# A chunked RWKV-7 state recurrence (WKV) inside a two-layer network: small transposes moved onto quarters of the matmul array, and side work moved to other steps

## What is computed

```python
def step(S, inp):                       # per token t and head (32 heads of 64 channels)
    r_t, w_t, k_t, v_t, kk_t, a_t = inp
    sa = jnp.einsum('bhvk,bhk->bhv', S, kk_t)
    S = (S * w_t[:, :, None, :]
         - sa[..., None] * (kk_t * a_t)[:, :, None, :]
         + v_t[..., None] * k_t[:, :, None, :])
    y = jnp.einsum('bhvk,bhk->bhv', S, r_t)
    return S, y
...
    mu = jnp.mean(y, -1, keepdims=True)
    yc = y - mu
    var = jnp.mean(yc * yc, -1, keepdims=True)
    y = (yc * lax.rsqrt(var + GN_EPS)).reshape(B, T, C) * gn_g + gn_b
```

## Time and profile before

| | |
|---|---|
| time, median of 3 runs | 2222.34 us (2221.25 to 2223.14) |
| time of the profiled execution | 2224.67 us |
| its span, first to last instruction | 2222.9 us |
| PE busy | 2170.7 us (98%) |
| the 16 steps, from the first key product to the first matmul of the output projection | 1506.98 to 1612.07 us, 105.09 us |
| granted PE clock over the span | 0.992 |

### The profile page before, as it was taken

The page is one execution under the profiler, slowest core; times in us unless marked ns, Lnnn a source line. Parts: engine busy times, 40 slices in busy tenths (PEclk is TensorE's granted clock), DMA queues, the critical chain, the costliest instruction groups (busy, mean ns, idle before and its releaser), DMA issues.

```text
span 2222.9 us, 38422 instructions
## 1 busy us (share of the span) xinstructions
PE 2170.7 (98%) x14720; PEld 1853.2 (83%) x14720; DVE 1486.3 (67%) x2054; ACT 1080.1 (49%) x1520; POOL 89.0 (4%) x78
## 2 busy tenths in 40 slices
PE   9999999999999999999899999998899999999997
PEld 7888888888888888888788887887688888888886
DVE  6656568885578856885875589784676644566655
ACT  5444555444444444445644755544434534456533
POOL 0700000000000000000000000001210000000000
PEclk9999999999999999999999999999999999999998
DMA  8655545665666656655464555653454555654552
GB/s 291 206 160 159 166 150 177 189 188 185 187 188 188 189 188 189 189 170 175 148 214 146 172 164 160 202 161 81 109 182 146 179 180 191 194 154 143 165 186 86
DMA packets 399585, 383.35 MB, mean 172 GB/s; under 512 B 43497, under 2 KB 397345, under 8 KB 398625
## 3 DMA queue, kind: packets, MB, share of 16 engines
q1 hardware_dynamic: 399458, 381.58, 55.7%
HBM read 374.65 MB, written 6.87 MB: 172 GB/s over the span
## 4 chain that ended last, share of the span: by engine, by line
PE 87%; DVE 8%; ACT 2%; issue 2%; DMA 1%; POOL 0%; DVEq 0%; SPq 0%; ACTq 0%; POOLq 0%
PE acc L793 45%; PE acc L796 22%; PE acc L824 3%; PE acc L879 2%; PE acc L880 2%; PE acc L881 2%; DVE w_lo L2072 2%; PE acc L827 2%; PE aux L1165 1%; ACT w_hi L1448 1%; PE aux L1074 1%; PE aux L896 1%; PE aux L1094 1%; DVE inverse L2508 0%; PE aux L1373 0%
## 5 line engine op out<-in xcount | busy, mean ns | idle before, releaser
L2072 DVE TENSOR_TENSOR w_lo<-raw_w,w_hi 128x1024 fp32r<-128x1024 f32 (+1 forms) x592 | 712.8, 1223 | 458.0 <-ACT w_hi L1448 456.4
L1448 ACT ACTIVATE w_hi<-raw_w 128x1024 fp32r<-128x1024 f32 (+1 forms) x592 | 613.6, 1046 | 674.7 <-PE acc L796 576.1
L793 PE MATMUL acc<-h,w_hi 128*128 128x512 f32 x1664 | 525.8, 397 | 1.2 <-DVE w_lo L2072 1.2
L796 PEld LDWEIGHTS acc<-h,w_lo 128*128 128x128 f32 x1664 | 312.6, 188 | 73.8
L796 PE MATMUL acc<-h,w_lo 128*128 128x256 f32 x1664 | 327.0, 278 | 0.0
L793 PEld LDWEIGHTS acc<-h,w_hi 128*128 128x128 f32 x1664 | 254.5, 189 | 2.1 <-issue 1.3
L793 PE MATMUL acc<-ff,w_hi 128*128 128x512 f32 x704 | 222.8, 398 | 2.4 <-DVE ff L2329 2.4
L793 PE MATMUL acc<-x_split,w_hi 128*128 128x512 f32 x704 | 225.2, 401 | 0.0
L793 PE MATMUL acc<-xs_b,w_hi 128*128 128x512 f32 x512 | 162.5, 399 | 1.7 <-DVE w_lo L2517 0.9
L796 PEld LDWEIGHTS acc<-ff,w_lo 128*128 128x128 f32 x704 | 133.0, 189 | 31.5
L796 PEld LDWEIGHTS acc<-x_split,w_lo 128*128 128x128 f32 x704 | 132.2, 188 | 31.2
(11 more groups left out here) (370 smaller groups left out, 3100.2 us busy)
## 6 DMA issues: line engine op xcount, KB each, us to landing
raw_w<-in_w_up SPq DMA_DIRECT2D x176, 512.0 KB, 3.5
raw_w<-in_a_w_in SPq DMA_DIRECT2D x128, 512.0 KB, 3.8
raw_w<-in_w_in SPq DMA_DIRECT2D x64, 512.0 KB, 4.0
raw_w<-in_w_down SPq DMA_DIRECT2D x64, 512.0 KB, 3.6
raw_w<-in_b_w_qg SPq DMA_DIRECT2D x64, 512.0 KB, 3.7
raw_w<-in_w_o SPq DMA_DIRECT2D x32, 512.0 KB, 3.6
raw_w<-in_a_w_out SPq DMA_DIRECT2D x32, 512.0 KB, 3.8
raw_w<-in_w_k_shared SPq DMA_DIRECT2D x32, 512.0 KB, 4.5
```

The source lines that it names most:

```text
L793: pe.matmul(ACC[2 * b + f], WHI[:, q, k, f * P:(f + 1) * P], op[:, kt, :, :].rearrange("p h t -> p (h t)"), start=first, stop=False)
L796: mm = pe.matmul(ACC[2 * b + f][:, 0:T], WLO[:, slot, k, f * P:(f + 1) * P], op[:, kt, 0, :], start=False, stop=last)
L1448: act.activation(WHI[:, u % 4, 0:ku, :], RAWW[:, u, 0:ku, :], ACT.Copy).then_inc(hi_made, 1)
L2072: dve.tensor_tensor(WLO[:, u, 0:ku, :], RAWW[:, u, 0:ku, :], WHI[:, u % 4, 0:ku, :].bitcast(F32), ALU.subtract)\
```

## The change

The tile transposes are done head by head: eight 64x64 matmuls in place of four with 128 rows, each on a quarter of the array, the two heads of a tile into two banks. To make room the state's sums go to the banks of X and U, so `x_first` has to wait until the sums are read, and comes after the second term of Y. `turn_beta` follows `turn_k` at once. `group_squares` moves ahead of `beta_pairs`, DVE's reading of its sums ahead of the copy of U. Weight units are split in other steps, and one `head_pair` and one `by_gate` per group come one and two steps later.

```diff
--- before.py
+++ after.py
@@ -477,14 +477,15 @@
 ...
-        PAIR_BANKS, KB_BANK, V_BANK = BANKS[:, 0:2, :], BANKS[:, 2, :], BANKS[:, 3, 0:T]
-        STATE_SUMS = BANKS[:, 3, T:].rearrange("p (e x) -> p e x", e=2)
-        XU_BANKS, Y_BANKS = SIDE[:, 0:2, :], SIDE[:, 2:4, :]
+
+        PAIR_BANKS, KB_BANKS, V_BANKS = BANKS[:, 0:2, :], BANKS[:, 2:4, 0:T], BANKS[:, 2:4, 384:]
+        XU_BANKS, Y_BANKS, STATE_SUMS = SIDE[:, 0:2, :], SIDE[:, 2:4, :], SIDE[:, 0:2, 384:]
 
         def by_two(x):
 
             return x.rearrange("p e (j t) -> p e j t", j=2)
-        SPLIT_AT = [5, 9, 13, 14]
+        SPLIT_AT = [6, 10, 14, 14]
+        LOW_SPLIT_AT = [10, 14, 15, 15]
 
 ...
@@ -754,7 +755,7 @@
                 g, c = STEPS[n]
                 if c == 3 and 0 < g < 3:
                     by_gate(2 * (g - 1))
-                if c == 0 and g > 1:
+                if c == 2 and g > 1:
                     by_gate(2 * (g - 2) + 1)
                 if c == 0 and g:
                     pool.wait_ge(gn_sq_sum, g)
@@ -1156,14 +1157,14 @@
             channel, between = (lambda h_, e: (h_, e)), (lambda h_, e: (h_ ^ e, e))
             across = lambda h_, e: (1 - e, h_)
 
-            def quads(banks, at, lhs, rhs, place, start, stop, one_bank=False):
+            def quads(banks, at, lhs, rhs, place, start, stop):
 
                 for j in range(2):
                     for e in range(2):
                         for h_ in range(2):
                             b, bank = place(h_, e)
                             mm = pe.matmul(banks[64 * b:64 * b + 64, bank, at + j * CHUNK:at + (j + 1) * CHUNK], lhs(h_, 2 * j + e), rhs(h_, 2 * j + e),
-                                           start=(start and j == 0 and not (one_bank and e == 1)), stop=(stop and j == 1 and (e == 1 or not one_bank)))
+                                           start=(start and j == 0), stop=(stop and j == 1))
                 return mm
 
 ...
@@ -1233,31 +1234,28 @@
                                        start=(i < 2), stop=(i >= 2))
                 mm.then_inc(prep_done, 1)
 
-            def tile_of(x, n, i):
-                g, c = STEPS[n]
-                return x[:, 4 * g + i, c * CHUNK:(c + 1) * CHUNK]
+            def turn_heads(banks, x, n, half, unit_, place):
+
+                for j in range(2):
+                    for e in range(2):
+                        for h_ in range(2):
+                            a, b = place(2 * j + e), half ^ e
+                            mm = pe.matmul(banks[64 * b:64 * b + 64, h_, a:a + CHUNK], at(x, n)(h_, 2 * j + e),
+                                           unit_[64 * h_:64 * h_ + 64, 64 * h_:64 * h_ + 64], start=(j == 0), stop=(j == 1))
+                return mm
 
             def turn_v(n):
                 if n:
                     pe.wait_ge(vt_out, 2 * n)
-                for i in range(4):
-                    b = i % 2
-                    mm = pe.matmul(V_BANK[64 * b:64 * b + 64, i // 2 * P:(i // 2 + 1) * P], tile_of(V, n, i), CENTRE, start=(i < 2), stop=(i >= 2))
-                mm.then_inc(tok_done, 1)
-
-            def turn(x, n, half):
-                for i in range(4):
-                    b = half ^ i % 2
-                    mm = pe.matmul(KB_BANK[64 * b:64 * b + 64, i * P:(i + 1) * P], tile_of(x, n, i), IDENT, start=True, stop=True)
-                return mm
+                    pe.wait_ge(kb_out, k_beta_turned(n - 1))
+                turn_heads(V_BANKS, V, n, 0, CENTRE, lambda i: i // 2 * CHUNK).then_inc(tok_done, 1)
 
             def turn_k(n):
-                if n:
-                    pe.wait_ge(kb_out, k_beta_turned(n - 1))
-                turn(K, n, 0)
+                pe.wait_ge(vt_out, 2 * n + 2)
+                turn_heads(KB_BANKS, K, n, 0, IDENT, lambda i: i * CHUNK)
 
             def turn_beta(n):
-                turn(BET, n, 1).then_inc(tok_done, 1)
+                turn_heads(KB_BANKS, BET, n, 1, IDENT, lambda i: i * CHUNK).then_inc(tok_done, 1)
 
             def group_squares(g):
 
@@ -1290,6 +1288,8 @@
                 m = n % 2
                 pe.wait_ge(pairs_read, n + 1)
                 pe.wait_ge(vt_out, 2 * n + 2)
+                if n:
+                    pe.wait_ge(s_taken, 3 * (n // NCH) + n % NCH)
                 mm = quads(XU_BANKS, 0, tok(k_kappa(m)), v_tok(m), between, True, n % NCH == 0)
                 mm.then_inc(x_begun if n % NCH else x_done, 1)
 
@@ -1316,40 +1316,37 @@
                     turn_v(n + 1)
                 pe.wait_ge(us_ready, 3 * n + 1)
                 quads(XU_BANKS, T, cross, far(US), between, True, True).then_inc(w_done, 1)
+                if c == 0 and g:
+                    group_squares(g - 1)
                 if more:
                     beta_pairs(n + 1)
                 if n:
                     pe.wait_ge(y_out, n)
                 if c > 0:
                     quads(Y_BANKS, 0, state, at(R, n), channel, True, False).then_inc(s_read, 1)
-                elif g:
-                    group_squares(g - 1)
                 pe.wait_ge(ws_ready, n + 1)
                 quads(XU_BANKS, P, inverse, mid(XS), across, True, True).then_inc(u_done, 1)
                 if state_next:
                     turn_k(n + 1)
+                    turn_beta(n + 1)
                 pe.wait_ge(us_ready, 3 * n + 3)
                 if c < 3:
                     pe.wait_ge(kb_out, k_beta_turned(n))
                     pe.wait_ge(vt_out, 2 * n + 4)
-                    quads(STATE_SUMS, 0, kb(m), vu(m), channel, True, True, one_bank=True).then_inc(s_done, 1)
-                if c == 3 and more:
-                    x_first(n + 1)
-                if state_next:
-                    turn_beta(n + 1)
-                if c < 3:
-                    x_first(n + 1)
+                    quads(STATE_SUMS, 0, kb(m), vu(m), channel, True, True).then_inc(s_done, 1)
                 pe.wait_ge(rest_out, n + 1)
                 if c == 0 and g:
                     pe.wait_ge(gn_read, g)
                 quads(Y_BANKS, 0, vu(m), rho(m), channel, c == 0, True).then_inc(y_done, 1)
+                if more:
+                    x_first(n + 1)
 
             k_pairs(0)
             turn_v(0)
+            beta_pairs(0)
+            x_first(0)
             turn_k(0)
             turn_beta(0)
-            beta_pairs(0)
-            x_first(0)
             for n in range(len(STEPS)):
                 step(n)
 
@@ -1867,13 +1864,14 @@
             def v_copies(n):
                 act.wait_ge(tok_done, v_turned(n))
                 for e in range(2):
-                    act.activation(v_and_u(n % 2)[64 * e:64 * e + 64, :, e, :, :],
-                                   V_BANK[64 * e:64 * e + 64, :].rearrange("p (j h t) -> p j h t", j=2, h=2), ACT.Copy).then_inc(vt_out, 1)
+                    act.activation(v_and_u(n % 2)[64 * e:64 * e + 64, :, e, :, :].rearrange("p j h t -> p h j t"),
+                                   by_two(V_BANKS[64 * e:64 * e + 64, :, :]), ACT.Copy).then_inc(vt_out, 1)
 
             def k_beta_copy(n):
                 if n % NCH < 3:
                     act.wait_ge(tok_done, v_turned(n) + 1)
-                    act.activation(k_and_beta(n % 2), KB_BANK, ACT.Copy).then_inc(kb_out, 1)
+                    act.activation(k_and_beta(n % 2).rearrange("p (i h t) -> p h i t", i=4, h=2),
+                                   KB_BANKS.rearrange("p h (i t) -> p h i t", i=4), ACT.Copy).then_inc(kb_out, 1)
 
             def in_slots(x):
                 return x[:, :, :].rearrange("p (e j) t -> p e j t", e=2)
@@ -1907,8 +1905,8 @@
                     k_beta_copy(n + 1)
                 if c == 1 and g:
                     head_rstd(g - 1)
-                if n in SPLIT_AT:
-                    split_unit(SPLIT_AT.index(n))
+                for u in heads_at(n, SPLIT_AT):
+                    split_unit(u)
 
             v_copies(0)
             k_beta_copy(0)
@@ -2567,6 +2565,10 @@
                     read_kappa(n + 1)
                 dve.wait_ge(w_done, n + 1)
                 dve.tensor_tensor(slots(XS), by_two(XU_BANKS[:, :, T:384]), slots(XS), ALU.add).then_inc(ws_ready, 1)
+                if c == 0 and g:
+                    dve.wait_ge(gn_sq_sum, g)
+                    dve.tensor_scalar(GROWS[:, 0, :].rearrange("p (e t) -> p e t", e=2), Y_BANKS[:, :, P:T], 1.0 / CHUNK, GN_EPS,
+                                      ALU.mult, ALU.add).then_inc(gn_read, 1)
                 dve.wait_ge(u_done, 2 * n + 2)
                 dve.tensor_copy(v_and_u(n % 2)[64:P, :, 0, :, :].rearrange("p j h t -> p h j t"), by_two(XU_BANKS[64:P, :, P:T])).then_inc(us_ready, 1)
                 if more:
@@ -2590,14 +2592,11 @@
                         dve.wait_ge(s_taken, 3 * g + 1)
                         dve.sem_inc(s_ready, 1)
                 if c == 0 and g:
-                    dve.wait_ge(gn_sq_sum, g)
-                    dve.tensor_scalar(GROWS[:, 0, :].rearrange("p (e t) -> p e t", e=2), Y_BANKS[:, :, P:T], 1.0 / CHUNK, GN_EPS,
```

(7 more changed lines are left out.)

## The result

The changed kernel takes **2225.19 us** (median of 20 runs, 2220.49 to 2228.4) against 2222.62 for the kernel before in 20 runs beside it: a ratio of 1.0013 with a 95% interval of 1.0007 to 1.0019. It is 2.6 us slower where I forecast 5.7 us faster, and the time lies outside my range.

The account below looks back on a forecast made before the run. The recurrence was taken as bound by a chain passing between engines, which no engine fills. Step, side, start and end terms summed to 8.3 us gained, less 2.6 for two clock falls: 5.7 faster, 2216.6 us, range 2212.5 to 2220.5.

Parts of the forecast that it names:

- Prices of the parts: Unit costs on PE: an old turn issues in 0.42 to 0.46 us, a new one taken as 0.24, from `beta_pairs`.
- Ordinary steps: Eight steps with c = 0 or 1: second inverse product to x_second 2.72 us instead of 3.07, 2.8 gained.
- slower: Clock falls in ordinary steps, 1.3 us each; seven cancel the gain, one in each of 15 steps gives 2233.5; chance 0.04.
- Rival 3: New turns no cheaper, 0.43 us each: K's and beta's end later in 11 steps, 2.9 less gain, 2219.5; chance 0.10.
- Rival 2: PE's wait for its own last group costs 0.3 us more in 12 steps with x_second: 2220.2; chance 0.16.
- c = 2: Four steps without turns of K and beta: 2.75 us before, 2.72 after, 0.1 gained in all.
- The side terms: Gains from moved side work: sums' reading 1.1 us, `head_pair` 1.3, roots and splits 0.6 and 1.7, clock 1.3.
- the clock of step 6: Granted clock of 0.53 for 3.41 us after step 6's long idle; it goes with the idle, 1.3 us gained.
- Step 3 to 4: Second inverse product to the next: 4.88 us instead of 5.45, 0.6 gained.
- End: After step 15 DVE makes two low halves, not one; some 0.6 of 1.22 us reaches PE as loss.
- Start: The first x_first stands ahead of K's turn: 0.2 us lost.
- The clock falls in steps 8 and 12: PE idles before the sums of squares, waiting for POOL; the clock then falls twice, 1.3 us lost each.

Follow-up runs that it names:

- experiment 1: Kernel before with only the moved side work (splits, gate work, `head_pair`, squares, reading of the sums), turns and order untouched: 2218.69 us against 2222.09, ratio 0.9989.
- experiment 5: Changed kernel with 32 tiny matmuls (128 PE instructions, half a block) put once ahead of the first turn of V: 2228.01 us against 2222.58, ratio 1.0019.
- Experiment 3: Changed kernel, new order and side work kept, with the old 128-row turns of K, beta and V: 2222.24 us, ratio 0.9997 to the kernel before.
- experiment 11: Changed kernel with the old turns, and ACT's first copy of k and beta put behind its first copy of x: 2220.41 us against 2222.75, ratio 0.9991.
- experiment 4: Kernel before with 16 tiny PE instructions added ahead of each turn of V and 32 ahead of each turn of K: 2230.72 us, ratio 1.0041.
- experiment 10: Kernel before with the side work moved, plus 32 tiny matmuls once ahead of the first turn of V: 2222.19 us against 2222.75, ratio 0.9997.
- experiments 6 and 7: 7 of 8 matmuls of the state's product with r left out: changed kernel 2219.64 us, 5.5 less; kernel before 2222.94 against 2222.58, ratio 1.0004.

## Why the prediction was wrong

**The step that failed** is a term that I never wrote down. Under "Prices of the parts" I priced a new turn by its duration alone, 0.24 us, and took its number of instructions, twice that of an old one, as free; under "Ordinary steps" this became "both turns are free", covered by the copy of U. That cover holds for PE's array, not for PE's supply of instructions: 640 more went into places that were already dense. The gaps inside groups took 12.35 us more than before, and the stretch got 3.65 longer. A term of up to 12 us was missing (at most, since part of a gap can lie beside a wait that would have been there anyway), and the rivals had no mechanism near it; "slower" stood for the clock alone.

By subtraction all else gained 12.35 - 3.65 = 8.7 us, close to my 8.3. That is luck. The steps below show over 2 us less than forecast for those with c < 3, and in steps 8 and 12 the gaps took the place of PE's wait for POOL's squares: from u1 to u2 it is 2.18 us there, against 3.07 in experiment 1.

The section of the Trainium skill named above says of crossing such a block's end that it is "mostly hidden". In the kernel before the trace agrees (1.20 us in 105); in the changed one it does not (13.55 us in 109).

By its steps:

- *Price of a turn, 0.24:* right. The turns at 1517.79 and 1518.03 in the rows below are 0.24 apart. Rival 3 falls. The rule of the Trainium skill that I quoted against the row doesn't agree with the new turns either: 16 matmuls in 0.24 us are 15 ns apart.
- *Ordinary steps, 0.35 each:* a third of that. The timeline of step 1 to 2 in the changed kernel, undisturbed by gaps:

```profile
1517.57 0.32 PEld L1166 LDWEIGHTS aux<-wkv_x,inverse_blocks 64*64 64x64 f32 x16
1517.79 0.33 PEld L1243 LDWEIGHTS acc<-consts,k 64*64 64x64 f32 x16
1518.03 0.33 PEld L1243 LDWEIGHTS acc<-consts,beta 64*64 64x64 f32 x16
1518.58 1.01 PEld L1166 LDWEIGHTS aux<-wkv_small 128*64 128x64 f32 x32 [0.22 <-DVE wkv_small L2573]
...
1519.85 0.45 PEld L1166 LDWEIGHTS aux<-wkv_small 64*64 64x64 f32 x16 [0.26 <-issue]
1520.52 0.32 PEld L1166 LDWEIGHTS aux<-wkv_s,r_kappa 64*64 64x64 f32 x16 [0.21 <-PE aux L1166]
...
1521.55 0.35 PEld L1166 LDWEIGHTS aux<-wkv_x,inverse_blocks 64*64 64x64 f32 x16 [0.37 <-issue]
```

  The sums start at 1.01 as forecast; x_first at 2.28 (2.21); x_second at 2.95 (2.72). x_second follows x_first by 0.67, not 0.51: PE's wait for its own group, which I put at 0.05, is named with 0.21, 2.56 us over the 12 steps. Rival 2 was half right. Old 3.07, new 2.95: 0.12 gained. For c = 2 it is a loss of 0.1 in place of a gain: from u2 to the next u1 3.88 in step 14, where no gap lies, against 3.80 before.
- *The side terms* (waits for the sums, `head_pair`, roots and splits, the clock of step 6: 1.1 + 1.3 + 0.6 + 1.7 + 1.3 = 6.0): the mechanisms are right, the match with the 6.04 of experiment 1 is in part luck. Of the 1.7 for step 6 only 0.95 came there, as its late turn of beta still holds up the root (u2 to u1 4.90, before 5.85); 0.86 came from gaps inside groups instead. In the changed kernel, with its earlier turn, u1 of step 6 waits 0.37 instead of 2.11.
- *Step 3 to 4, 4.88 from u2 to u2:* right where no gap lies; experiment 5 has 4.83, against 5.45.
- *End, 0.6 lost for the second low half:* right. From the first matmul of the output projection to the one behind the next low half it is 16.04 us in the changed kernel and 16.06 in experiment 1, against 15.34 before, since PE now waits for the root:

```profile
1624.86 0.23 PEld L1281 LDWEIGHTS aux<-head_rstd_rows,consts 32*64 32x64 f32 x16 [1.41 <-ACT head_rstd_rows L1883]
```

- *Start, 0.2 lost:* about right (3.88 us from the first load to u1, against 3.71), but only since the new turns are short. Experiment 3 shows 1.0 for the same order, and the copy ahead of x's, which I didn't look at, is a likely reason but not a shown one (experiment 11).
- *The clock falls in steps 8 and 12:* wrong for the changed kernel. The gaps delay PE, so that POOL's squares are there in time: the sums of squares go at once at 1560.68. The clock fell in step 13 instead, behind a gap (busy windows of the changed kernel, 0.69 over 5.5 us):

```profile
1594.50:1600.00 5.50, 4.49 (x141) 4.11 (x137) 1.56 (x4) 1.95 (x5) 0.58 (x1) 0.69 0.12 20
```

  Without the gaps there the wait comes back, and once the fall with it. In experiment 5, step 12:

```profile
1590.55 0.58 PEld L1265 LDWEIGHTS aux<-group_norm_squares,consts 128*32 128x32 f32 x16 [1.39 <-POOL group_norm_squares L764]
```

  The granted clock is 0.50 from 1590.66 to 1594.07. In step 8 of that run, and in both steps of experiment 1 with 3.07 from u1 to u2, no fall came: the wait was forecast rightly, the clock only as one outcome of several.

The parts in this order: before 2222.1; side work -3.4 (2218.7); the new order +3.5 (2222.2); the new turns +3.0 (2225.2). Each difference is uncertain by some 2 us, as the intervals are about 0.1% to either side.

**Open:** why a block can be used only 1.2 to 1.6 us after its packet has landed; what sets the start of a packet, 1.2 to 3.0 us after the gap before it; whether other transfers lengthen the gaps by lengthening the packets (0.92 to 1.47 us; not tried); and why the spells of low clock outside the stretch differ from kernel to kernel.

## What to carry to other kernels

Count PE's instructions as well as its time: where a change makes many small matmuls of few large ones, look for the place where some 253 matmuls and weight loads pass fastest, and if that comes well under 4 us, PE may stop in the middle of groups (13 times at 3.00 us, three times at 3.75, never at 3.50 in experiment 4). Where it stops hangs on where the blocks end, so a small shift of the stream can change the loss. The sign in a profile is "issue" idle inside a group, at counts that differ by whole blocks, each ending just behind a packet of the instruction queue. A change of several parts is worth running part by part: here the half that moved side work was the whole gain, 3.4 us, and it alone is worth keeping, though experiment 10 shows how easily such a gain goes.

## What the runs showed of the hardware that I had not expected

- PE's instruction stream comes in packets of 16 KB, and stops of 0.3 to 1.7 us lie at whole multiples of 252.7 counted instructions, each ending 1.2 to 1.6 us after a packet, in places where PE would pass a block in under about 4 us (an estimate from gaps that end 3.9 to 5.2 us apart).
- A PE group that waits for PE's own last group starts 0.67 us behind that one's start, 0.21 of it named as idle, where without a wait the next group follows by 0.24.
- 28 instructions in each of 12 steps cost 5.5 us in one stream and nothing in another (experiments 6 and 7).
